# Where the normed token tiles of a decoder trunk are transposed: DMA crossbar in place of TensorE

## The reference, cut to what matters

```python
def rmsnorm(x, g):
    y = xf * lax.rsqrt(jnp.mean(xf * xf, axis=-1, keepdims=True) + EPS)
    return (y * g.astype(jnp.float32)).astype(x.dtype)

def layer(x, ...):
    h = rmsnorm(x, g_pre_mix)
    z = h @ w_in                       # pool a | sgu u | sgu v | gate_a | gate_b, 4608 columns
    ...
    m = jax.nn.sigmoid(ga) * (ya @ w_ba) + jax.nn.sigmoid(gb) * (yb @ w_bb)
    x = x + rmsnorm(m @ w_out, g_post_mix)
    f = jnp.square(jax.nn.relu(rmsnorm(x, g_pre_ffn) @ w_up)) @ w_down
    x = x + rmsnorm(f, g_post_ffn)
```

## Time and profile before

| | |
|---|---|
| median of 3 runs | 3743.42 us (3743.28 to 3745.61) |
| the profiled execution | 3744.18 us |
| span of its slowest core, which the rows show | 3742.8 us (the eight cores: 3735.5 to 3742.8) |
| busy on that core | PE 3669.6 us (98%), DVE 1767.3 (47%), ACT 1158.8 (31%), POOL 542.1 (14%) |
| granted TensorE clock, mean | 0.994 to 0.995 of full speed on every core |
| DMA | 449.32 MB moved; the weight queue alone takes 61.0% of the 16 engines' span |

### The profile page before, as it was taken

One profiled execution on the slowest core, in us unless ns is written; L12 is line 12 of the kernel. 1 busy time (PEld: TensorE's weight loads), 2 busy tenths in 40 slices (PEclk: granted clock), 3 DMA queues, 4 the chain that ended last, 5 costly groups with the idle time before them and its releaser, 6 DMA issues.

```text
span 3742.8 us, 63960 instructions; the slowest of 8 cores (3735.5 to 3742.8 us)
## 1 busy us (share of the span) xinstructions
PE 3669.6 (98%) x22208; PEld 2101.6 (56%) x22208; DVE 1767.3 (47%) x3385; ACT 1158.8 (31%) x2528; POOL 542.1 (14%) x1220
## 2 busy tenths in 40 slices
PE   6999999999999999999999999999999999999999
PEld 3554555555455555545555554554665565665664
DVE  3642652563355256335525624642652652652652
ACT  2331332323233232323323332331332332332331
POOL 1111110211111121011101101111111111111110
PEclk9999999999999999999999999999999999999999
DMA  8684665567466566756655665685877777777773
GB/s 167 100 150 72 121 116 95 100 113 144 79 123 127 94 148 113 134 94 111 123 92 100 111 119 102 104 148 110 166 144 127 142 137 125 145 138 125 137 123 84
DMA packets 75338, 449.32 MB, mean 120 GB/s; under 512 B 9488, under 2 KB 11152, under 8 KB 29072
## 3 DMA queue, kind: packets, MB, share of 16 engines
q0 software_dynamic: 57600, 385.48, 61.0%
q1 hardware_dynamic: 17424, 59.76, 5.2%
HBM read 817.55 MB, written 13.10 MB: 222 GB/s over the span
## 4 chain that ended last, share of the span: by engine, by line
PE 94%; DVE 2%; issue 1%; ACT 1%; DMA 1%; POOL 1%; DVEq 0%; SPq 0%; ACTq 0%; POOLq 0%
PE ps L391 85%; PE ps L925 6%; PE ps L448 2%; PE ps L814 1%; ACT R L402 1%; DMA trilT<-c_tril 1%; DMA x<-xp 0%; DVE x L1016 0%; DVE ps L822 0%; POOL stt L418 0%; POOL stt L413 0%; ACT hst L431 0%; ACT junk L1006 0%; ACT L402 0%; DVE R L802 0%
## 5 line engine op out<-in xcount | busy, mean ns | idle before, releaser
L391 PE MATMUL ps<-hTb,wslot 128*128 128x384 bf16 (+1 forms) x11520 | 1859.1, 319 | 11.0 <-DVE hTb L454 4.2
L391 PEld LDWEIGHTS ps<-hTb,wslot 128*128 128x128 bf16 x11520 | 1122.3, 98 | 657.0 <-issue 25.4
L391 PE MATMUL ps<-wslot,R 128*128 128x512 bf16 x4352 | 947.6, 379 | 0.0
L402 ACT ACTIVATE R<-ps 128x384 bf16<-128x384 f32 (+5 forms) x1208 | 574.6, 482 | 916.6 <-PE ps L391 851.9
L391 PEld LDWEIGHTS ps<-wslot,R 128*128 128x128 bf16 x4352 | 424.1, 98 | 502.7
L943 DVE TENSOR_TENSOR R<-R 128x384 bf16<-128x384 bf16 (+1 forms) x768 | 266.3, 347 | 587.3 <-ACT R L402 585.5
L391 PE MATMUL ps<-R,wslot 128*128 128x384 bf16 (+1 forms) x2304 | 414.0, 318 | 1.3 <-DVE R L834 1.2
L312 POOL DMA_DIRECT2D wslot<-wslab x359 | 203.5, 568 | 951.9 <-PE ps L391 719.0
L402 ACT ACTIVATE sg<-ps 128x384 bf16<-128x384 f32 (+1 forms) x384 | 179.8, 471 | 491.4 <-PE ps L391 246.5
L391 PEld LDWEIGHTS ps<-R,wslot 128*128 128x128 bf16 x2304 | 225.0, 98 | 132.0 <-issue 6.7
L996 DVE TENSOR_TENSOR R<-ps,gpost 128x512 f32<-128x512 f32 x68 | 47.0, 692 | 432.2 <-ACT junk L993 432.2
(11 more groups left out here) (75 smaller groups left out, 1824.1 us busy)
## 6 DMA issues: line engine op xcount, KB each, us to landing
wslot<-wslab POOLq DMA_DIRECT2D x359, 1024.0 KB, 15.6
x<-xp SPq DMA_DIRECT2D x16, 512.0 KB, 5.9
yp<-x SPq DMA_DIRECT2D x16, 512.0 KB, 7.2
gpre<-g_pre_m SPq DMA_DIRECT2D x12, 512.0 KB, 12.8
R<-b_sp SPq DMA_DIRECT2D x12, 512.0 KB, 13.3
gpre<-g_pre_f SPq DMA_DIRECT2D x12, 512.0 KB, 12.5
gpost<-g_pm SPq DMA_DIRECT2D x12, 512.0 KB, 15.9
gpost<-g_pf SPq DMA_DIRECT2D x12, 512.0 KB, 4.3
```

The lines of the kernel that those rows point to most:

```text
L391: r = e.matmul(ps[b][:, 0:N], lhsT=lh, rhs=rh, start=(at + q == 0), stop=(at + q == total - 1))
L402: lambda e: e.activation(out=out, in_=in_, func=func, **kw), cost=act_us(N))
```

## The change

130 of the 136 tiles take another way from `hst` to `hT`: one DMA on SP's queue, `dma_start_transpose`, which writes all of `hT[:, :, tile]` from `hst`. Their eight TensorE transposes, their PSUM bank and their DVE copy are gone. The six tiles of the very first norm (block 0, layer 0) keep the TensorE way (`by_pe`). `hst` has four buffers in place of three. The planner's estimate for such a DMA is 1.5 us of cost and 5.0 us of latency.

```diff
+    def dma(self, reads, writes, out, in_, cost=1.5, lat=2.0, transpose=False):
...
+        return self.op("sp", reads, writes, lambda e: (e.dma_start_transpose if transpose else e.dma_start)(out=out, in_=in_),
+                       semkey=key, inc=16, extra=(prev,) if prev[1] > 0 else (), cost=cost, lat=lat)
...
-        hst = [sb(f"hst{i}", [128, 1024], BF16) for i in range(3)]
+        hst = [sb(f"hst{i}", [128, 1024], BF16) for i in range(4)]
...
+        def norm_tail(i, k, hT, by_pe=False):
+            q = nxt("hst", 4)
...
+            if not by_pe:
+                yield S.ready(("hst", q)), False
+                S.dma([("hst", q)], [("hT", i)], hT[:, :, i * 128:(i + 1) * 128], hst[q][:, :], lat=5.0, transpose=True)
+                return
             yield S.ready(("hst", q)) + 0.3, True
...
-            launch(i, lambda i=i: start_norm(i, xslot(0, i), views(768)["hT"]))
+            launch(i, lambda i=i: start_norm(i, xslot(0, i), views(768)["hT"], True))
```

More of the change, by code:

```diff
@@ L112, in ready @@
         return max(self.done.get(self.lw[k], 0.0) for k in keys) + 0.12
-    def dma(self, reads, writes, out, in_, cost=1.5, lat=2.0):
+    def dma(self, reads, writes, out, in_, cost=1.5, lat=2.0, transpose=False):
         i = self.ring
@@ L118, in dma @@
         prev = (key, self.val[key])
-        return self.op("sp", reads, writes, lambda e: e.dma_start(out=out, in_=in_), semkey=key, inc=16,
-                       extra=(prev,) if prev[1] > 0 else (), cost=cost, lat=lat)
+        return self.op("sp", reads, writes, lambda e: (e.dma_start_transpose if transpose else e.dma_start)(out=out, in_=in_),
+                       semkey=key, inc=16, extra=(prev,) if prev[1] > 0 else (), cost=cost, lat=lat)
     def finish(self):
@@ L424, in add_eps @@
                                               op0=ALU.add))
-        def norm_tail(i, k, hT):
-            q = nxt("hst", 3)
+        def norm_tail(i, k, hT, by_pe=False):
+            q = nxt("hst", 4)
             CH.flush(hst_chain.get(q))
@@ L455, in norm_tail, with start_norm @@
                                          in_=pT16.rearrange("p (c t) -> p c t", c=8)), cost=dve_us(1024, 2))
-        def start_norm(i, k, hT):
+        def start_norm(i, k, hT, by_pe=False):
             yield S.ready(("x", k)), False
-            yield from norm_tail(i, k, hT)
+            yield from norm_tail(i, k, hT, by_pe)
         def launch(i, gen_fn):
```

## The result

The changed kernel is slower: ratio 1.0675 to the kernel before, 95% interval 1.0659 to 1.0691, so about 3996 us against 3743.6 (+253 us). In three of the change's seven runs one die worked at a lower clock and they took 4280 us or more, which says nothing of the change; the other four took 3992.3 to 3999.5 us. The prediction said 3863 us.

A forecast was written before the change was run, and what follows sets the result against it. TensorE (PE), busy 98% of the span, was taken as the bound. A 52.0, B 66.4, C 28.0 and boundaries 32.0, less 58.5 us off PE, gave +119.9: 3863 us against the median, range 3715 to 4010.

The forecast's parts named there:

- L: Time from the end of a tile's `hst` to the tile landed by DMA; taken as 9 us, ends 2.6 and 12.6.
- the room: Time a tile's DMA has before PE waits: reader's start minus 0.9 us minus end of `hst`.
- A: Tile 2 in the middle of a six-tile layer, 8 times: room 4.2 us, forecast cost 52.0 us with half clock.
- B: Tile 5 in the middle of a six-tile layer, 8 times: room 2.4 us, forecast cost 66.4 us with half clock.
- C: Tile 2 in a five-tile layer, 4 times: room 3.7 us, forecast cost 28.0 us with half clock.
- boundaries: Two block boundaries: tile 2's DMA waits behind earlier transfers on SP's queue, gaps of 21.2 and 11.8 us; net 32.0 together.
- old gap for tile 5: At the first block boundary: the existing 2.67 us gap, 4.4 with its clock loss, was to disappear.
- half clock: After a PE gap of about 2.67 us or longer: largely 1.2 GHz in place of 2.4, 1.7 us lost each.
- the row of the gains: Load of 512 KB of gains issued just after B's `hst`, behind two weight slabs: took 12.6 us.
- The case that I called much slower: Rival: many small packets each wait for a slab's, L about 18 us, 4051 us in all; chance 0.15.
- All this is hidden: Ends of layers, tiles 0 to 2 and tile 4 in five-tile layers: room long enough, so no wait counted.
- The faster case: Rival: crossbar packets few or large, burst hardly delays them; L below 4.7 us, 3719 us at 2.6; chance 0.24.

## Why the prediction was right in direction and wrong in size

The mechanism was the one predicted: L beats the room, and PE waits in front of the up groups. The size was off by a factor of two. Waits in us, forecast against measured, with the half clock apart:

| term | forecast | measured |
|---|---|---|
| A, 8 times | 38.4 (4.8 each) | 51.2 (5.6 to 8.4 each) |
| B, 8 times | 52.8 (6.6) | 108.6 (11.7 to 16.9) |
| C, 4 times | 21.2 (5.3) | 29.9 (6.6 to 8.5) |
| tile 4, five-tile layers, 4 times | 0, "hidden" | 29.9 (4.4 to 10.0) |
| boundaries | 33.0 (21.2 and 11.8) | 45.6 (20.0 and 25.7) |
| ends of layers | 0 | 8.5 in four |
| old gap for tile 5, ACT and weight waits gone | -2.7 | -10 |
| half clock | 35.7 | 49.1 |
| taken off PE | -58.5 | -58.5 (taken over) |
| sum | 119.9 | 254.3 |

The sum is that of the spans, 3997.1 - 3742.8. The last two measured entries are not apart in the trace: PE's busy time fell by 9.4 us, which with 58.5 taken off leaves 49.1 for the half clock. Most of it shows in one row, the matmuls that read `hTb` and so follow the gaps (before, then after), 41.1 us longer:

```profile
L391 PE MATMUL ps<-hTb,wslot 128*128 128x384 bf16 (+1 forms) x11520 | 1859.1, 319 | 11.0 <-DVE hTb L454 4.2
```

```profile
L391 PE MATMUL ps<-hTb,wslot 128*128 128x384 bf16 (+1 forms) x11520 | 1900.2, 324 | 279.9 <-DMA hTb<-hst 273.6
```

The four gaps at the ends of layers, 1.7 to 2.5 us, have full clock (1.00) behind them, so it is 1.9 for each of the other 26; I had read 1.7. The run without weights, at 0.995 clock, has 66.5 us less of busy PE than the kernel before, but 180 of its 21,168 matmul records are missing, which by the idle time that no wait explains (16.5 us, 7.0 in the change) is worth some 9 us. That leaves about 57 for the transposes, so 58.5 is about right.

**The step that failed** is "I take **L = 9 us** at A, B and C". By wait plus room, L was 10.6 at A and 11.2 at C, not far off, but 16.0 at B, and the landing times from the issue say much the same (10.0, 9.5 and 16.0). B alone, forecast at 52.8 and measured at 108.6, is 56 of the 134 us by which the sum was short. There I had set the row of the gains, 12.6 us, aside "because a tile has half the bytes"; yet the row of 30 KB beside it had said that bytes do not count, and the two slabs issued just ahead of B's tile are named in the same paragraph. Even the row of the gains would have been short: the gains behind B's tile took 15.1 and 15.7 us in the change. The case that I called much slower (L about 18, because a tile is many small packets) was nearer at B: 66 packets on each engine. But the packets as such are worth only some 70 of the 274 us, and little of it stands at A and C (5.8 us less and 6.6 more): "the number of packets of a transposing DMA decides" does not hold there. The Trainium skill ("DMA: Bandwidth & Descriptors", section Queues, rings and completion order) has each engine go round its queues packet by packet. The runs agree that fewer packets wait less, but not in proportion: with 9 in place of 66, waits of 200 in place of 270 us.

**Also wrong: "All this is hidden"**, for tile 4 in the five-tile layers. Its room is long, but four slabs are issued together at 3254.2, just behind C's gap and 1.5 us ahead of its DMA (issued at 3255.7), and it landed 30 us after that. In the kernel before the slabs at this place went out as two pairs 3.7 us apart (3323.9 and 3327.6); that C's gap gathered them is argued from this, no run shows it by itself.

**The boundaries**: at the first the number was right (20.0 for 21.2) and its reason wrong. With the tile on another queue the wait stays, and without weights it goes. It is the slabs again, not the store and the load ahead; at the second, where I priced the tile by the store, 25.7 came for 11.8.

**Right**: the copies taken off DVE changed nothing that PE waits for, weights did not starve, and the clock after a gap was priced well. The faster case, L below 4.7, is refuted under load and true without: 3.0 to 3.1 us. The Trainium skill ("Advanced Engine Details and Errata", section X-Bar Transpose (TRN2)) holds that transposing DMAs are as fast as ordinary ones, and the run with plain copies in as many packets agrees (waits of 267 and 274 us). The 0.7 us that I had estimated from its bandwidth is not what a tile takes: the least landing is 3.0 us. My other estimate, 10.5 us for eight times the 1309 ns of one block in the Trainium skill ("VectorE: DVE Perf Modes", section The three transpose paths), doesn't hold here either: a whole tile of eight blocks lands in 3.0 us where no slab is under way.

**Open**: why 9 packets still take 10.5 us under the slabs at B, and which part of the wait is spent at the reading and which at the writing side. No run here tells.

## What to carry to other kernels

Read the latency of a small DMA from a row that lies under the same traffic at the same moment, and one for each place: the median over a run (7.2 us here) hides 3.0 and 30. Before a path is moved from a busy engine to the DMA, look what is issued in the microseconds ahead of it; if bulk loads with slack stand there, hold them or let fewer go, but no longer than their slack lasts. And work taken off the bounding engine can change the order of what stays: 85 tiles off PE gave next to nothing, because a group that had covered a copy no longer stood between the transposes and their reader.

## What the runs showed that I had not expected

The issue of such a DMA can hold its engine. One tile's DMA instruction in after, all 130 of it (ns min/median/max, first and last start):

```profile
L119 SPq DMA_TRANSPOSE hTb<-hst x130: 1216/1297/15189, 167.1 to 3843.6; - x130
```

And the plain copy, in runs of 256 B and in rows of 2 KB:

```profile
L119 SPq DMA_DIRECT2D hTb<-hst x130: 593/594/9648, 168.5 to 3848.0; - x130
```

```profile
L119 SPq DMA_DIRECT2D hTb<-hst x130: 464/465/701, 168.6 to 3771.3; - x130
```

The transposing DMA takes 1.3 us to issue and up to 15 under the slabs; without weights it is 2.3 at most. A plain copy in about as many packets takes 0.6 us and up to 9.6, with 9 packets 0.5 and never more than 0.7. So the long holds come with the many packets under the slabs, and the transposing form adds to the usual time. At the first boundary it kept the next store from being issued for 13 us (1418.92 to 1432.06 in the timeline above). On ACT's queue the same thing held an engine that evicts PSUM, for up to 18 us.
